# Attention scores in two passes on 128 rows, and gates moved into the attention stages

## The reference

```
h = rmsnorm(x);  proj = h @ w_in
q_sb, k_sb, v_sb, q_dl, k_dl, v_dl, gate_pre = split(proj)
g_sb, g_dl = sigmoid(gate_pre + b)                     # 2 x 1024 wide
# stick-breaking, 8 heads of 64:
z = q_sb k_sb^T / 8;  a = exp(log_sigmoid(z) + sum of log_sigmoid(-z) between key and query)
y_sb = (a v_sb) @ w_sb_out                             # strictly causal
# dilated windows, 4 KV heads x 3 groups (stride 1, 4, 16), rope on q and k:
y_dl = (softmax mixture over the groups, times v_dl) @ w_dil_out
x = x + (g_sb * y_sb + g_dl * y_dl) @ w_o
```

## Time and profile before

| what | value |
|---|---|
| median of 3 runs | 1127.26 us (1125.91 to 1127.86) |
| the profiled execution | 1127.22 us, span 1125.3 us |
| PE busy | 1101.4 us, 98% |
| DVE busy | 770.2 us, 68% |
| ACT busy | 543.7 us, 48% |
| first FFN, mixing layer up to `w_o`, rest | about 363, 353 and 409 us |
| scores of the first head to the first dilated scores | 381.4 to 525.2 us |
| dilated stage | 525.2 to 661.3 us |
| end stage (`gdl`, `dil`) | 661.3 to 716.3 us |

### The profile page before, as it was taken

The page is one execution under the profiler, slowest core; times in us unless marked ns, Lnnn a source line. Parts: engine busy times, 40 slices in busy tenths (PEclk is TensorE's granted clock), DMA queues, the critical chain, the costliest instruction groups (busy, mean ns, idle before and its releaser), DMA issues.

```text
span 1125.3 us, 15594 instructions
## 1 busy us (share of the span) xinstructions
PE 1101.4 (98%) x6033; PEld 943.5 (84%) x6033; DVE 770.2 (68%) x1090; ACT 543.7 (48%) x870; POOL 2.7 (0%) x6
## 2 busy tenths in 40 slices
PE   8999999999999999999999999999999999999996
PEld 6888899988998788877777778788898899889985
DVE  7876378745868778678765556667774578637864
ACT  6554155523644456567755543425552355415642
POOL 0000000000000000000000000000000000000000
PEclk9999999999999999999999999999999999999999
DMA  8323233332324212111112113422233323333222
GB/s 295 96 75 113 75 113 113 113 94 94 93 73 131 79 39 75 56 38 53 51 57 75 52 57 96 142 94 94 90 104 106 95 94 113 94 94 113 82 68 75
DMA packets 34295, 103.18 MB, mean 92 GB/s; under 512 B 4144, under 2 KB 7472, under 8 KB 34224
## 3 DMA queue, kind: packets, MB, share of 16 engines
q1 hardware_dynamic: 34224, 102.21, 28.9%
HBM read 100.10 MB, written 2.10 MB: 91 GB/s over the span
## 4 chain that ended last, share of the span: by engine, by line
PE 85%; DVE 6%; ACT 4%; issue 3%; SPq 1%; DMA 1%; POOL 0%; POOLq 0%; DVEq 0%; ACTq 0%
PE acc_pair L1208 24%; PE acc_pair L1209 24%; PE acc_pair L1210 24%; PE pair_bank L1208 2%; PE pair_bank L1210 2%; PE pair_bank L1209 2%; DVE w_lo L785 1%; PE bank L1208 1%; PE bank L1210 1%; PE bank L1209 1%; ACT rope L646 1%; ACT w_hi L487 1%; DMA w_raw<-in_w13a 1%; PE bank L1216 1%; PE bank L1218 1%
## 5 line engine op out<-in xcount | busy, mean ns | idle before, releaser
L1208 PE MATMUL acc_pair<-xg_hi,w_hi 128*128 128x512 f32 (+1 forms) x693 | 265.5, 383 | 1.5 <-DVE w_lo L1016 1.5
L1209 PE MATMUL acc_pair<-xg_lo,w_hi 128*128 128x512 f32 (+1 forms) x693 | 259.8, 375 | 0.0
L1210 PE MATMUL acc_pair<-xg_hi,w_lo 128*128 128x512 f32 (+1 forms) x693 | 259.1, 374 | 0.0
L487 ACT ACTIVATE w_hi<-w_raw 128x1024 fp32r<-128x1024 f32 (+3 forms) x159 | 154.3, 976 | 147.9 <-PE acc_pair L1210 147.3
L785 DVE TENSOR_TENSOR w_lo<-w_raw,w_hi 128x1024 fp32r<-128x1024 f32 (+3 forms) x159 | 178.6, 1126 | 42.3 <-ACT w_hi L487 41.3
L1210 PEld LDWEIGHTS acc_pair<-xg_hi,w_lo 128*128 128x128 f32 x693 | 130.5, 188 | 24.6
L1208 PEld LDWEIGHTS acc_pair<-xg_hi,w_hi 128*128 128x128 f32 x693 | 130.8, 189 | 23.1 <-issue 2.8
L1209 PEld LDWEIGHTS acc_pair<-xg_lo,w_hi 128*128 128x128 f32 x693 | 131.0, 189 | 19.9 <-issue 0.7
L1210 PE MATMUL acc_pair<-hid_hi,w_lo 128*128 128x512 f32 x352 | 138.8, 394 | 0.0
L1209 PE MATMUL acc_pair<-hid_lo,w_hi 128*128 128x512 f32 x352 | 138.2, 393 | 0.0
L1208 PE MATMUL acc_pair<-hid_hi,w_hi 128*128 128x512 f32 x352 | 136.9, 389 | 0.0
(11 more groups left out here) (220 smaller groups left out, 2059.7 us busy)
## 6 DMA issues: line engine op xcount, KB each, us to landing
w_raw<-in_w13b SPq DMA_DIRECT2D x44, 512.0 KB, 3.6
w_raw<-in_w13a SPq DMA_DIRECT2D x40, 512.0 KB, 3.8
w_raw<-in_wmix SPq DMA_DIRECT2D x22, 512.0 KB, 3.5
w_raw<-in_w2a SPq DMA_DIRECT2D x16, 512.0 KB, 3.6
w_raw<-in_w2b SPq DMA_DIRECT2D x16, 512.0 KB, 3.5
w_raw<-in_wgate SPq DMA_DIRECT2D x8, 512.0 KB, 3.5
w_raw<-in_wend SPq DMA_DIRECT2D x8, 512.0 KB, 3.5
w_raw<-in_wo SPq DMA_DIRECT2D x8, 512.0 KB, 3.5
```

Source lines behind the costliest of these rows:

```text
L487: act.activation(w_hi[:, s, 0:width], w_raw[:, s, 0:width], ACT.Copy).then_inc(whi_done, 1)
L1208: pe.matmul(o, w_h, r_h, start=first, stop=False, skip_group_check=check)
L1209: pe.matmul(o, w_h, r_l, start=False, stop=False, skip_group_check=check)
L1210: return pe.matmul(o, w_l, r_h, start=False, stop=last, skip_group_check=check)
```

## The change

It has five parts.

1. *Scores in two passes.* For each head a tile of 128 rows is kept. The queries' tile `sq2` holds their high part in the head's own 64 rows and their low part in the other 64. The keys' tile `sk2` holds the high part in its own rows and the same again (its twin, copied by a DMA) in the others. One pass of 128 rows then gives `hi*hi + hi*lo`. A second pass takes `sk_lo`, the keys' low part with zeros in the other rows, set once by POOL. The dilated tiles `dq2`, `dk2`, `dk_lo` are made alike. Each high and low part of q, k, rq and rk is now made by two instructions of 64 rows, one per head. The two twin DMAs of a key stand in SP's queue ahead of the load of the unit seven places later, behind a wait for the key's high parts.
2. *An edit of the suffix step.* The high part of `ebuf` is made by ACT, not DVE.
3. *The order.* Keys are projected ahead of queries. One more half unit stands ahead of the first scores (5 instead of 4), and fins and half units fall at other places of the list. Three first gates come after `rv0`, inside stick-breaking, and are kept in `gsb_tiles`; the other five go into the tiles of rope (`rope2`, `roped`, `cos`, `sin`), which are free by then. The tanh of the early gates waits until the last head's suffix step, where the table of functions is exchanged anyway.
4. *Four of the second gates* (`gdl` 0 to 3) are half units of the dilated stage. The first five dilated blocks have three half units each, the other eleven two.
5. *The end stage* has four `gdl` left and all eight `dil`, in the order of `END_ORDER`, written out and no longer as a loop.

```diff
-MIX_ORDER = ([("q", 0, 0), ("k", 0, 0), ("v", 0, 0), ("q", 1, 0), ("k", 1, 0), ("v", 1, 0), ...
+PROJ = ([("k", 0, 0), ("q", 0, 0), ("v", 0, 0), ("k", 1, 0), ("q", 1, 0), ("v", 1, 0),
+         ("rk", 0, 0), ("k", 2, 0), ("q", 2, 0), ("v", 2, 0), ("rq", 0, 0), ("rq", 0, 1),
+         ("k", 3, 0), ("q", 3, 0), ("v", 3, 0), ("rq", 0, 2), ("rv", 0, 0)]
+        + [("rk", 1, 0)] + [("rq", 1, g) for g in range(NG)] + [("rv", 1, 0)])
+FIRST = 17
+EARLY_GATES = 3
+EARLY_DL = 4
+MIX_ORDER = (PROJ[0:FIRST] + [("gate", m, 0) for m in range(EARLY_GATES)] + PROJ[FIRST:] + [("sb", 0, 0)]
+             + [u for m in range(EARLY_GATES, KD) for u in (("gate", m, 0), ("sb", m - EARLY_GATES + 1, 0))]
+             + [("gdl", 0, 0), ("sb", 6, 0), ("gdl", 1, 0), ("sb", 7, 0), ("gdl", 2, 0), ("gdl", 3, 0)])
+END_ORDER = [("gdl", 4), ("dil", 0), ("dil", 1), ("dil", 2), ("gdl", 5), ("dil", 3), ("dil", 4), ("gdl", 6),
+             ("dil", 5), ("dil", 6), ("gdl", 7), ("dil", 7)]
-SB_FILL = ((3, 1), (1, 1), (4, 1), (2, 2), (4, 1), (3, 1), (2, 2), (1, 1))
-DL_FILL = (2,) * 16
+SB_FIRST = 5
+SB_FILL = ((3, 1), (1, 1), (4, 1), (2, 2), (4, 1), (3, 1), (2, 2), (3, 1))
+DL_FILL = (3,) * 5 + (2,) * 11
...
 # SP
+                if u - 7 in KEYS:
+                    sp.wait_ge(op_hi_done, split_parts(nth(u - 7) + 1))
+                    for head in (0, 1):
+                        key = stacked(u - 7, head).bitcast(F32)
+                        sp.dma_start(key[head_rows(head + 1), :], key[head_rows(head), :]).then_inc(twin_done, 16)
...
 # ACT, fin
-                    act.activation(dst, src, ACT.Copy).then_inc(op_hi_done, 1)
+                        for head in (0, 1):
+                            rows = head_rows(head)
+                            act.activation(stacked(w, head)[rows, :], src[rows, :], ACT.Copy).then_inc(op_hi_done, 1)
...
 # ACT, suffix
+                    for b in range(3):
+                        cols = slice(SB_AT[b], SB_AT[b] + SB_WIDTH[b])
+                        act.wait_ge(a_done, 3 * w + b + 1)
+                        act.activation(spA_hi[:, cols], ebuf[:, cols], ACT.Copy).then_inc(a_hi_done, 1)
...
 # DVE, fin
+                        for head in (0, 1):
+                            rows, hi = head_rows(head), stacked(w, head)
+                            lo = hi[head_rows(head + 1), :] if what == "q" else sk_lo[rows, pair % 2, head, :]
+                            dve.tensor_tensor(lo, src[rows, :], hi[rows, :].bitcast(F32),
+                                              ALU.subtract).then_inc(op_lo_done, 1)
...
 # PE, scores
+                    pe.wait_ge(twin_done, 32 * (KEYS.index(MIX + MIX_ORDER.index(("k", hp, 0))) + 1))
-                            product(o, sk_hi[rows, hp % 2, ks], sk_lo[rows, hp % 2, ks],
-                                    sq_hi[rows, hp % 2, P * i:SEQ], sq_lo[rows, hp % 2, P * i:SEQ],
-                                    n == 0, False, True)
+                            pe.matmul(o, sk2[:, hp % 2, a, ks], sq2[:, hp % 2, a, P * i:SEQ], start=n == 0,
+                                      stop=False, skip_group_check=True)
+                            pe.matmul(o, sk_lo[:, hp % 2, a, ks], sq2[:, hp % 2, a, P * i:SEQ], start=False,
+                                      stop=False, skip_group_check=True)
...
 # PE, dscores
-                    product(bank[0], dq_hi[jp][rows, 0, own], dq_lo[jp][rows, 0, own], dk_hi[jp][rows, :],
-                            dk_lo[jp][rows, :], True, False, True)
+                    for g in range(NG):
+                        o = bank[1][:, (g - 1) * P:g * P] if g else bank[0]
+                        keys = own if g else slice(0, SEQ)
+                        pe.matmul(o, dq2[jp][:, a, g, own], dk2[jp][:, a, keys], start=g < 2, stop=False,
+                                  skip_group_check=True)
+                        mm = pe.matmul(o, dq2[jp][:, a, g, own], dk_lo[jp][:, a, keys], start=False, stop=g != 1,
+                                       skip_group_check=True)
```

More of the change, by code:

```diff
@@ L75 @@
 OUT_POOL = (0, 1)
-GATE_COLS = ((0, 1024), (1024, 512))
-END_COLS = ((0, 1024), (1024, 256))
+GATE_COLS = {"gate": slice(0, 1024), "sb": slice(1024, 1536)}
+END_COLS = {"gdl": slice(0, 1024), "dil": slice(1024, 1280)}
 SB_BANKS = (((1, 0), (3, 384)), ((2, 0),), ((0, 0),))
@@ L84, in chunk_base, with unit_kind, is_proj @@
     return base + sum(2 * n + KD for _, n in CHUNKS[:c])
+def unit_kind(u):
+    return MIX_ORDER[u - MIX] if u < END else END_ORDER[u - END]
+def is_proj(u):
+    return MIX <= u < END and unit_kind(u) in PROJ
 def unit_width(u):
@@ L113, in mix_schedule, with tanh @@
     halves = [(half, u) for u in range(MIX, END)
-              for half in (("Us",) if u >= GATE and (u - GATE) % 2 else ("Ua", "Ub"))]
+              for half in (("Us",) if unit_kind(u)[0] == "sb" else ("Ua", "Ub"))]
+    tanhs = []
+    def tanh():
+        while tanhs:
+            s.append(("tanh", tanhs.pop(0)))
     def fill(n):
@@ L119, in fill @@
             s.append((half, u))
-            if MIX < u <= GATE and half == ("Ub" if MIX_ORDER[u - 1 - MIX][0] in ("rq", "rk") else "Ua"):
+            if is_proj(u - 1) and half in ("Us", "Ub" if unit_kind(u - 1)[0] in ("rq", "rk") else "Ua"):
                 s.append(("fin", u - 1))
-            if half == "Ub" and u >= GATE:
+            if half == "Ub" and unit_kind(u)[0] in ("gate", "gdl"):
                 s.append(("gate", u))
+                tanhs.append(u)
+                if ("suffix", 2 * SB_PAIRS - 1) in s:
+                    tanh()
             if half == "Us":
@@ L129, in mix_schedule @@
     s.append(("norm", 1))
-    fill(4)
+    fill(SB_FIRST)
     s.append(("scores", 0))
@@ L174, in mix_kind, with nth, split_parts @@
     return MIX_ORDER[u - MIX]
+def nth(u):
+    return PROJ.index(mix_kind(u))
 def through(*units):
-    return max(MIX_ORDER.index(u) for u in units) + 1
+    return max(PROJ.index(u) for u in units) + 1
+def split_parts(n):
+    return sum(1 if what in ("v", "rv") else 2 for what, _, _ in PROJ[:n])
+KEYS = [u for u in FINS if mix_kind(u)[0] in ("k", "rk")]
 ROPES = [u for u in FINS if mix_kind(u)[0] in ("rq", "rk")]
@@ L378, in gsb, with gate_at @@
         def gsb(m):
-            return gsb_tiles[:, KD - 1 - m, :]
+            if m < EARLY_GATES:
+                return gsb_tiles[:, m, :]
+            return (rope2[:, 0, :], rope2[:, 1, :], roped[:], cos[:], sin[:])[m - EARLY_GATES]
+        def gate_at(u):
+            what, m = unit_kind(u)[0:2]
+            if what == "gate":
+                return gsb(m)
+            return gd_tiles[:, m, :] if m < EARLY_DL else gdl[:, m % 2, :]
         def wait_lo(engine, u0, i):
@@ L399, in reads @@
         def reads(u0, i):
-            n = len([u for u in range(u0 % RING, u0, RING) if not MIX <= u < GATE])
+            n = len([u for u in range(u0 % RING, u0, RING) if not is_proj(u)])
             return n + i
@@ L1225, in bank_free @@
                     return
-                if not MIX <= last < GATE:
+                if not is_proj(last):
                     pe.wait_ge(acc_read[u0 % RING], reads(u0, i))
@@ L1462, in _ @@
                     mm.then_inc(pv_done, 1)
-            with pe.Fori(0, KD // 4) as i:
-                for j in range(0, 8, 2):
-                    unit(END + j, 2 * i, xg, K8)
-                    if j == 0:
+            for u in range(END, WO):
+                what, m = unit_kind(u)
+                if what == "gdl":
+                    unit(u, 0, xg, K8)
+                else:
+                    if m == 0:
                         pe.wait_ge(ys_done, 2 * (SB_PAIRS + DL_PAIRS))
-                    unit(END + j + 1, 2 * i, yd, K8[0:DL_PAIRS])
+                    unit(u, 0, yd, K8[0:DL_PAIRS])
             for m in range(KD):
@@ L1537 @@
     first = {"q": 0, "k": SBT, "v": 2 * SBT, "rq": 3 * SBT, "rk": 3 * SBT + DQT, "rv": 3 * SBT + DQT + DL_PAIRS}
-    order = [first[what] + DL_PAIRS * g + pair for what, pair, g in MIX_ORDER]
+    order = [first[what] + DL_PAIRS * g + pair for what, pair, g in PROJ]
     gate0 = first["rv"] + DL_PAIRS
```

231 lines of the change are left out of this document (120 added, 111 removed).

## The result

The changed kernel takes 1133.0 us (median of 6 runs, 1131.9 to 1134.1) against 1127.3 for the kernel before on the same chip: ratio 1.005, 95% interval 1.0037 to 1.0063. It is 5.8 us slower, where the forecast was 2.8 us faster, and it lies above the range. The profiled run took 1133.1 us with a span of 1131.3.

A forecast was written before the change was run, and what follows sets the result against it. TensorE (PE), busy 98% of the span, bounds the kernel: 1127.2 - 12.2 - 6.2 - 2.2 - 1.6 - 8.5 (waits now) + 6.2 + 11.4 + 2.6 + 7.7 = 1124.4 us. The 8-in-10 range was 1111 to 1132.

The forecast's parts named there:

- Passes and switches: Scores of dilated blocks and stick-breaking heads: removed passes save 12.2 us, removed 64-row switches 6.2 and 2.2.
- Rival C: Score passes: the switch is no matter of rows, so 8.4 us of gain goes, 1132.8 us; chance 0.05.
- The start: Before the first scores: the wait of 1.2 us goes, and the slow clock of 1.6 us with it.
- Stick-breaking: Attention heads: PE waits 6.2 us in three places, against 2.5 now; the largest, 2.4, at scores(5).
- Dilated blocks: Blocks 1, 2 and 3: PE waits 4.5, 2.4 and 4.5 us, together 11.4, against 2.6 now.
- Last PV: End of the dilated stage: the last PV waits behind a tanh, 2.6 us instead of 1.7.
- End stage: Before gdl(5), gdl(6), gdl(7) and the first `wo`: PE waits 7.7 us, against 0.5 now.
- Waits in all: PE's waits from stick-breaking to the end stage: 6.2 + 11.4 + 2.6 + 7.7 us, against 8.5 now.
- The clock: Start of the mixing layer: the fall from 384.3 to 387.5 goes, 1.6 us; the sum adds no other falls.
- Rival B: Clock falls behind the new waits: 1130 us with two falls, 1138 with four and longer waits; chance 0.19.
- Rival A: Queues run ahead, so PE waits for only part of the 28 us charged: 1113 us; chance 0.31.
- Rival D: Keys' twin DMAs before the scores: late in most heads, +10 us, 1134 us; chance 0.03.

The follow-up runs named there:

- run 5: Changed kernel with one high copy and one low part of 128 rows per q, k and rope unit, not two of 64 rows each: 1121.6 us.
- run 6: Changed kernel with the high part of the weights after the suffix sums made by DVE again, not ACT: 1135.6 us.
- run 7: Changed kernel with GpSimd making the high copy of the second head's 64 rows beside ACT's copy of the first: 1129.4 us.
- run 12: Kernel before (three passes on 64 rows, single parts, no twins) with the changed order and ACT's high parts after the suffix sums: 1137.1 us.
- run 3: Changed kernel with 16, 20, 20 and 9 extra matmuls on PE in the waits of scores(5), dilated blocks 1 and 3, last PV: 1129.4 us.
- run 13: Kernel of run 8 with 14 extra matmuls ahead of the transposes of dilated block 1: 1116.6 us.
- run 15: Kernel of run 8 with one half unit moved from between suffix(6) and scores(7) to between scores(7) and suffix(7): 1116.1 us.
- run 8: Changed kernel with the old order of steps and gates put back and GpSimd making the second head's high copies: 1116.6 us.

## Why the prediction was wrong

Each of the three parts was measured in more than one state of the others:

| part | measured |
|---|---|
| two passes, old order, single parts | 1126.9 to 1113.8: -13.1 |
| two passes, changed order, single parts | 1137.1 to 1121.6: -15.5 |
| doubled parts, old order | 1113.8 to 1124.2: +10.4 |
| doubled parts, changed order | 1121.6 to 1133.0: +11.5 |
| order, three passes | 1126.9 to 1137.1: +10.2 |
| order, two passes, single parts | 1113.8 to 1121.6: +7.8 |
| order, as changed | 1124.2 to 1133.0: +8.9 |

The way from 1126.9 by 1113.8 and 1124.2 to 1133.0 adds up by construction. What the runs show is that each part keeps its size, within some 2.5 us, when the others change. The rows that start at 1126.9 also hold the keys ahead of the queries, the extra half unit and ACT's copy. Each theory named about half of the loss.

Step by step:

- **Passes and switches**: right in kind, too small in size. 24.4 us by groups and heads against 20.6; the switch for masks takes 0.1 behind a mask and nothing ahead of it. Rival C is refuted: beside each other, f32 passes of 128 rows have no stretch. The Trainium skill, "TensorEngine Tiling (Array Packing)", "Key Properties", says that a change of tiling mode drains TensorE; the traces agree, and its price was the 0.39 us per group of the earlier trace rows.
- **The start**: the fall at 384 went. A wait of 1.1 us from start to start stayed, for `raw` instead of the low part. Minor.
- **Stick-breaking**: right places, wrong size. Waits from start to start are 8.8 us against 6.2: scores(5) 3.8 us, where I had 2.4.
- **Dilated blocks**: 4.7, 1.8 and 4.9 us, with 4.5, 2.4 and 4.5 forecast; 12.0 against 11.4 from start to start. Right, also in cause: single parts take 1.2 to 2.6 off blocks 1 and 3.
- **Last PV**: 2.6, right. **End stage**: 7.1 against 7.7, right, and the same whatever the parts and passes are (waits of 2.4, 1.3, 1.3 and 1.3 us in runs 5, 6, 7 and 12 as in the changed kernel).
- **Waits in all**: 31.6 against 27.9. This is the places added up, small stretches beside them included. Summed from PE's pitches, waits over 0.5 us alone went from 7.8 to 30.6 us.
- **The clock**: this is the step that failed. The sum took 1.6 us off for the fall that goes and put nothing in for falls behind the waits it had itself forecast, though the earlier trace rows showed one behind a wait of 1 us. There are four in the mixing layer, 8.1 us, and 0.6 us for one at the kernel's end: 8.7 us where the sum has nothing. Keeping PE busy (run 3) took 4.8 of it away and gave back 3.7 in the time.

So -24.4 - 1.6 - 8.5 + 31.6 + 8.7 = +5.8, of 6.0 between the spans. Against the forecast, the passes brought 3.8 us more and the waits cost 3.7 us more; that these two cancel is luck. What is left of the miss of 8.7 us (1133.1 against 1124.4) is the clock. This is an account of PE's queue; runs 13 and 15 show that a fall taken away can come back as a wait. Rival B was the true case, at a chance of 0.19: four falls, and 3.7 us more of waits. It gave 1130 for two falls and 1138 for four with waits a quarter longer, at 1.6 us a fall; here a fall cost 1.4 to 3.2 us. The only argument against it, that waits of 1.4 and 1.6 us were followed by no fall, could not speak for waits of 4. Rival A failed as its own objection said: the chains are dependent steps. Rival D never showed in the changed kernel.

What decided beyond the clock was in the sum, but not seen as what it was: the order. 7.7 us of the end stage and part of the dilated waits are the price of gates moved away; what they should cover moved with them, since a filler that makes PE arrive later also makes ACT and DVE work earlier. The old order with GpSimd's half copies, 1116.6 us, is 1.5% faster than the changed kernel (from the medians) and 1.0% faster than the kernel before (0.9886 to 0.9919).

Open: why waits of equal length are followed by a fall in one run and not in another; whether the order could be rearranged as a whole, with every unit's end placed against the softmax, below 1116.

## What to carry to other kernels

A filler of the bottleneck engine is not only cover. It has an end on the other engines, and moved forward it puts that end ahead of the chain that it should hide: write each engine's queue for the new order, and price the stage that the filler left.

When you cut passes on the bound engine by preparing its operands better, price the preparation on the chains it waits for. Here 24 us of matmul became 13 even with free operands, and doubled copies of 0.63 us on engines that were half idle took 10 of these.

Where your own sum contains waits of 2 to 5 us on TensorE, put the clock behind each of them into the sum, not into a rival. But read the next wait before you pay to avoid a fall: in runs 13 and 15 one followed, and the time was the same with and without the fall.

## What the runs showed of the hardware

- 64 rows cost ACT as much as 128: `dq` copies take 629 ns of 64 rows in the changed kernel and 631 ns of 128 in run 5.
- GpSimd copies 64 x 512 to fp32r in 0.61 us, and in 1.43 to 1.55 when DVE began an operation with two SBUF operands 0.15 us earlier (five of 16 copies in run 8). A low part of DVE that begins during a copy on GpSimd takes 0.98 to 1.10 us instead of 0.69.
- The length of a wait alone does not tell whether the clock falls behind it. Ahead of gdl(5) the same 2.36 us were followed by a fall in run 3 and by none in the changed kernel.
- Falls differ in length: in the changed kernel PE worked at the lower level for 6.3 us behind scores(5) and for 2.8 behind the wait of 4.9 us at dilated block 3.
- Going from f32 to a bf16 mask on the same 128 rows takes nothing, coming back 0.1 us.
